# A fused two-block forward pass: compact 32x32 inverse in the scan, packed queries, and a reordered end of the branch stage

## The reference, cut to what matters

```python
# first block, per direction (forward and backward) and head: a scan over tokens
sa = einsum('bhij,bhj->bhi', S, a_t)
S = S * w_t[:, :, None, :] + sa[..., None] * b_t[:, :, None, :] + v_t[..., None] * k_t[:, :, None, :]
y = einsum('bhij,bhj->bhi', S, r_t)
# first block, queries: 8 heads of 64 plain and 32 rotated columns
q = einsum('blr,rf->blf', rms_norm(u_mla[..., :384]), w_uq).reshape(B, L, 8, 96)
q = concatenate([q[..., :64], rope_axial(q[..., 64:], *rot)], -1)
# second block, two layers:
proj = einsum("btd,de->bte", rms_norm(h), w_in[l])        # q k v, indexer, rnn, conv, gates
attn = dsa_attention(...)                                 # top-64 keys per query
rnn  = rg_lru_branch(...)
cnv  = silu(layer_norm(depthwise_conv31(a * sigmoid(g)))) # conformer branch
merged = g_attn*(attn@w_o_attn) + g_rnn*(rnn@w_o_rnn) + g_conv*(cnv@w_o_conv)
h = h + merged @ w_out[l]
h = h + (silu(f@w_gate) * (f@w_up)) @ w_down
```

## Time and profile before

| | |
|---|---|
| median of 3 runs | 1744.97 us (1736.07, 1744.97, 1745.1) |
| the profiled execution | 1739.31 us, its span 1737.5 us |
| mean granted clock of TensorE | 0.985 |
| PE busy | 1675.0 us, 96%, 14722 records |
| DVE busy | 1147.8 us, 66% |
| POOL busy | 661.8 us, 38% |
| ACT busy | 552.7 us, 32% |
| chain that ended last | PE 87%, DVE 6%, ACT 3% |
| largest parts of the chain | L783 18%, L740 16%, L1048 15%, L1072 8%, L2531 5% |

### The profile page before, as it was taken

How to read it: one execution, slowest core, us unless ns; L and a number is a source line. 1 busy time by engine, 2 the same in 40 slices (tenths; PEclk the granted TensorE clock), 3 DMA queues, 4 the chain that set the end, 5 groups by cost and what they waited for, 6 DMA issues and landing times.

```text
span 1737.5 us, 35985 instructions
## 1 busy us (share of the span) xinstructions
PE 1675.0 (96%) x14722; PEld 1480.8 (85%) x14722; DVE 1147.8 (66%) x2044; ACT 552.7 (32%) x1244; POOL 661.8 (38%) x581
## 2 busy tenths in 40 slices
PE   6999988999999999999999999999999998999999
PEld 3777646888889888878989999989888888999999
DVE  5646155665368789787757664368788896676643
ACT  3232363443343453433330010233554304120100
POOL 1535003554035122115645554164123046445652
PEclk9999996999999999999999999999999999999999
DMA  9333100000443444324344444443343343444543
GB/s 371 137 112 115 65 1 2 5 4 5 182 160 122 146 146 146 122 101 142 124 143 173 168 164 158 164 146 128 120 169 127 137 145 107 162 170 170 170 158 110
DMA packets 53379, 225.71 MB, mean 130 GB/s; under 512 B 5088, under 2 KB 29024, under 8 KB 29280
## 3 DMA queue, kind: packets, MB, share of 16 engines
q1 hardware_dynamic: 53216, 223.40, 36.8%
HBM read 222.34 MB, written 1.05 MB: 129 GB/s over the span
## 4 chain that ended last, share of the span: by engine, by line
PE 87%; DVE 6%; ACT 3%; DMA 1%; issue 1%; DVEq 1%; POOL 0%; SPq 0%; ACTq 0%
PE PS L783 18%; PE PS L740 16%; PE PS L1048 15%; PE PS L1072 8%; PE PS L2531 5%; PE PS L2643 3%; PE PS L2060 2%; PE PS L2073 2%; DVE arena L1455 2%; DMA ring<-stream_dram 1%; PE PS L722 1%; PE PS L2736 1%; PE PS L900 1%; PE PS L863 1%; PE PS L1012 1%
## 5 line engine op out<-in xcount | busy, mean ns | idle before, releaser
L783 PE MATMUL PS<-arena,ring 128*128 128x272 f32 (+1 forms) x1664 | 390.0, 389 | 0.3 <-DVE arena L1683 0.3
L783 PEld LDWEIGHTS PS<-arena,ring 128*128 128x128 f32 x1664 | 311.7, 190 | 59.7 <-issue 6.1
L1455 DVE SCALAR_TENSOR_TENSOR arena<-arena,par 128x272 f32<-128x272 f32 (+1 forms) x480 | 259.5, 599 | 7.4 <-issue 0.9
L1895 POOL TENSOR_TENSOR arena<-ring 128x512 f32<-128x512 f32 x48 | 68.7, 1431 | 443.8 <-DMA ring<-stream_dram 353.9
L740 PE MATMUL PS<-arena,ring 128*128 128x136 f32 (+1 forms) x1536 | 202.0, 280 | 1.4 <-ACT arena L1158 1.4
L740 PEld LDWEIGHTS PS<-arena,ring 128*128 128x128 f32 x1536 | 192.7, 191 | 8.1 <-ACT arena L1158 1.7
L740 PE MATMUL PS<-arena 128*128 128x136 f32 (+1 forms) x1152 | 147.9, 280 | 4.5 <-ACT arena L1138 3.0
L1048 PE MATMUL PS<-arena 128*128 128x136 f32 (+1 forms) x1280 | 152.1, 277 | 0.0
L1048 PEld LDWEIGHTS PS<-arena 128*128 128x128 f32 x1280 | 148.7, 191 | 0.0
L740 PEld LDWEIGHTS PS<-arena 128*128 128x128 f32 x1152 | 140.0, 191 | 5.8 <-POOL arena L1895 1.7
L1048 PE MATMUL PS<-arena,ring 128*128 128x136 f32 (+1 forms) x960 | 116.1, 277 | 0.0
(11 more groups left out here) (417 smaller groups left out, 2966.3 us busy)
## 6 DMA issues: line engine op xcount, KB each, us to landing
ring<-stream_dram SPq DMA_DIRECT2D x185, 1024.0 KB, 4.9
ring<-stream_dram SPq DMA_DIRECT2D x32, 512.0 KB, 4.0
ring<-stream_dram SPq DMA_DIRECT2D x16, 384.0 KB, 3.8
arena<-x_dram SPq DMA_DIRECT2D x1, 2048.0 KB, 8.3
cst<-const_dram SPq DMA_DIRECT2D x1, 1080.0 KB, 7.0
out_dram<-H SPq DMA_DIRECT2D x4, 256.0 KB, 3.1
cst<-const_dram SPq DMA_DIRECT2D x1, 912.0 KB, 12.7
arena<-stream_dram SPq DMA_DIRECT2D x1, 512.0 KB, 11.1
```

Of the source, the lines that this page charges most:

```text
L783: last = mm(PS[:, 2 * (j % 2) + f, nw], w[:, k, P * f:P * f + P], src[:, k, nw], start=k == 0, stop=k == KD - 1)
L1455: stt(CVG[:, c, NQ], CVA[:, c, j + Q0:j + T2], dw_w[l][:, c, j:j + 1], CVG[:, c, NQ], ALU.mult, ALU.add)
L1895: g.tensor_tensor(to[:, 0], w21, w22, ALU.add).then_inc(L["summed"], 1)
```

## The change

Three parts.

**Queries**: the eight heads' features are made as two groups of three full 128-row tiles (18 products instead of 24); ACT cuts them into heads with nine copies. The keys come before the swap, the swap's four products go to four different quarters of the partitions of one bank, DVE multiplies them in one instruction, and ACT moves them back. The gate rows and their addition move into the attention loop.

**Scan**: the 64x64 inverse is kept as its two 32x32 diagonal blocks, stored one above the other (ZW has 32 columns). Levels 1 to 4 work on 32x32 tiles, 32 products of 16 columns where 16 of 32 columns were; level 5 makes the corner, and PE copies the second block through an identity (FOLD); the whole inverse is put together in ZF. `grow` is no longer interleaved. `first_products` leaves out a corner that nobody needs.

**Layers**: step 12 becomes a mixed step. The convolution's pieces lie in other steps, with a table for each layer. The attention's token sums move from POOL to DVE (step 35 or 33). The layer norm begins at step 36 in the first layer, 37 in the second; squares, silus and the gains before the feed-forward part are cut in halves and put between the copies on ACT.

```diff
-CONV_SUM_J = 37
-MIXED = [*range(2, 8), 9, 11, 15, ...
-CONV_STEPS = {8: 3, ... 26: 1, 27: 4, 28: 5, 29: 3, 30: 5, 31: 5, 32: 3, 33: 4,
-              34: 4, 35: 5, 36: 1}
+CONV_SUM_J, ATT_SUM_J = (36, 37), (35, 33)
+MIXED = [*range(2, 8), 9, 11, 12, 15, ...
+CONV_STEPS = [{8: 3, ... 26: 1, **late}
+              for late in ({27: 4, 28: 8, 29: 3, 30: 7, 31: 5, 32: 3, 33: 4, 34: 4, 35: 1},
+                           {27: 5, 28: 5, 29: 6, 30: 8, 31: 6, 32: 4, 33: 3, 34: 2})]
...
-        ZW = lend(12, 2, 2, 2, 4, CH)
+        ZW, ZF = lend(12, 2, 2, 2, 4, 32), lend(14, 2, 2, 4, CH)
...
+                    if j == CONV_SUM_J[l] + 1:
+                        square(0)
+                    if j == CONV_SUM_J[l] + 4:
+                        conv_silu(1).then_inc(L["conv_out"], 1)
                     if j - 1 in MIXED:
                         copy_e(j - 1)
+                    if j >= WO_J + 2:
+                        gain(j - 2, (0,))
                     copy_g(j)
...
+                if j == ATT_SUM_J[l]:
+                    dve.wait_ge(L["o_kept"], B["o_kept"] + len(R))
+                    x = AT.rearrange("p (k e) t -> p k e t", e=2)
+                    token_sums(v, x[:, :, 0], x[:, :, 1], TATT, n0, n1).then_inc(L["att_halves"], 1)
...
-                if j == OA_J:
-                    pool.wait_ge(L["o_kept"], B["o_kept"] + len(rounds(l)))
-                    front_halves(pairs(AT), TATT, n0, n1, L["att_halves"])
-                    back_halves(pairs(AT), TATT, n0, n1, L["att_halves"])
...
                 for q, h in each:
-                    last = mm(PS[halves(h), 4 * d, 32 * q:32 * q + 32], XL[l - 1][halves(h), d, q, :],
-                              columns(ZW[halves(h), n % 2, d, 0, q, :], l, GROWN[d]), start=True, stop=True)
+                    if l < 5:
+                        for i in range(2):
+                            o = quad_of(h, i)
+                            last = mm(PS[o, 4 * d, 16 * q:16 * q + 16], XL[l - 1][o, d, q, :],
+                                      columns(ZW[o, n % 2, d, 0, q, :], l, GROWN[d]), start=True, stop=True)
+                    else:
+                        o = quad_of(h, 1 - d)
+                        last = mm(PS[quad_of(h, d), 4 * d, 32 * q:32 * q + 32], AS[n % 2][o, d, q, far(d)],
+                                  ZW[o, n % 2, d, 0, q, :], start=True, stop=True)
...
-                last = mm(PS[halves(h), 4 * d, 256 + 32 * q:288 + 32 * q], ZW[halves(h), n % 2, d, 1, q, :],
-                          P1[halves(h), d, 32 * q:32 * q + 32], start=True, stop=True)
+                n_out = 16 if l < 5 else 32
+                for q, h in each:
+                    for i in range(2):
+                        o, at = quad_of(h, i), slice(n_out * q, n_out * q + n_out)
+                        if l < 5 or i == d:
+                            w, src = ZW[o, n % 2, d, 1, q, :], P1[o, d, at]
+                        else:
+                            w, src = FOLD[o, :], ZW[o, n % 2, d, 0, q, :]
+                        last = mm(PS[o, 4 * d, 256 + at.start:256 + at.stop], w, src, start=True, stop=True)
...
                 for d in range(2):
+                    if n < NCH:
+                        grow(n, l, d)
+                for d in range(2):
                     for q, h in each:
-                        if n < NCH:
-                            grow(n, l, d, q, h)
                         if l == 1 and m >= 0:
                             value(m, d, q, h)
...
-            for i in range(KD):
-                last = mm(PS[:, 7, 2 * i:2 * i + 2], ROWSG[:, i // 2, P * (i % 2):P * (i % 2) + P], SEL, start=True, stop=True)
-            last.then_inc(gate_rows, 1)
...
-            for h in range(8):
-                if h >= 4:
-                    pe.wait_ge(mq_kept, h - 3)
-                for k in range(3):
-                    w = weights(UQ + h // 4, 3, 384)
-                    last = mm(PS[0:96, h % 4, 0:TX], w[:, k, 96 * (h % 4):96 * (h % 4) + 96], REST[:, 4 + k, :],
-                              start=k == 0, stop=k == 2)
+            for i in range(3):
+                for g in range(2):
+                    w = weights(UQ + g, 3, 384)
+                    for k in range(3):
+                        last = mm(PS[:, i, TX * g:TX * g + TX], w[:, k, P * i:P * i + P], REST[:, 4 + k, :],
+                                  start=k == 0, stop=k == 2)
...
+            for i in range(4):
+                last = mm(PS[32 * i:32 * i + 32, 4, :], perm32[64:96, :],
+                          QM[64:96, 2 * i:2 * i + 2, :].rearrange("p h t -> p (h t)"), start=True, stop=True)
```

More of the change, by code:

```diff
@@ L1261, in keep_gates, with square, conv_silu, gain @@
                       ).then_inc(L["ga_kept"], 1)
-            def gain(j):
-                for k in (2 * (j - WO_J), 2 * (j - WO_J) + 1):
+            def square(i):
+                act.wait_ge(L["conv_cent"], B["conv_cent"] + 1)
+                return a(CSQ[:, 4 * i:4 * i + 4, NQ], CVG[:, 4 * i:4 * i + 4, NQ], ACT.Square)
+            def conv_silu(i):
+                act.wait_ge(L["conv_normed"], B["conv_normed"] + 1)
+                for k in range(4 * i, 4 * i + 4):
+                    last = a(CVG[:, k, NQ], CVG[:, k, NQ], ACT.Silu, bias=q2l["ln_b"][:, k:k + 1],
+                             scale=q2l["ln_g"][:, k:k + 1])
+                return last
+            def gain(j, tiles=(0, 1)):
+                for k in (2 * (j - WO_J) + f for f in tiles):
                     act.wait_ge(L["mixed"], B["mixed"] + k + 1)
@@ L2254, in keep_solved, with keep_corner @@
                 last.then_inc(S["u_kept"], 1)
+            def keep_corner(n, d):
+                S = SCAN[d]
+                act.wait_ge(S["z_ready"], 4 * n + 4)
+                for h in range(2):
+                    o = quad_of(h, d)
+                    a(ZF[o, n % 2, d, :, far(d)], ZW[o, n % 2, d, 0], ACT.Copy)
             def keep_turned(n, d):
@@ L2278, in scalar_scan @@
                     if l == 5 and n < NCH:
+                        for d in range(2):
+                            keep_corner(n, d)
                         keep_turned(n, 0)
@@ L2307, in pool_scan @@
                 m = n - 1
-                for l in range(1, 6):
+                for l in range(1, 5):
                     for d in range(2):
@@ L2355, in first_inverse @@
                 dve.wait_ge(S["first_masked"], n + 1)
-                tt(w, w, over(eye, 4), ALU.add).then_inc(S["first_summed"], 1)
+                tt(w, w, over(FOLD, 4), ALU.add).then_inc(S["first_summed"], 1)
             def first_turned(n, d):
@@ L2704, in _ @@
                        start=True, stop=True).then_inc(ms_made, 1)
+                if i == 3:
+                    pe.wait_ge(vt_kept, 4)
+                    for f in range(KD):
+                        last = mm(PS[:, 7, 2 * f:2 * f + 2], ROWSG[:, f // 2, P * (f % 2):P * (f % 2) + P], SEL,
+                                  start=True, stop=True)
+                    last.then_inc(gate_rows, 1)
                 if i >= 3:
@@ L2885, in _ @@
                 a(KM[0:64, h, :], PS[halves(h % 2), h % 4, :], ACT.Copy).then_inc(mk_kept, 1)
+            act.wait_ge(lat_normed, 2)
+            for i in range(4):
+                last = a(PM[64:96, i, :], TURNED[quad[i], :], ACT.Copy)
+            last.then_inc(lat_root, 1)
             for t in range(4):
```

198 lines of the change are left out of this document (108 added, 90 removed).

## The result

The changed kernel takes 1774.28 us (median of 4 runs, 1772.95 to 1777.93), the kernel before 1744.57 (4 runs, 1736.07 to 1745.1). The ratio is 1.0185 with a 95% interval of 1.015 to 1.022: slower by 1.9%, where I had forecast 1703. The mean granted clock fell from 0.985 to 0.960.

The account below looks back on a forecast made before the run. PE was taken as the bound, busy 96% of the span. Queries −7, scan −15 and layers −17 sum to −39 from 1739.31 us, giving 1700 and, 3 us above, forecast 1703; range 1682 to 1741.

Parts of the forecast that it names:

- the scan's sum: Scan: shorter bursts minus growths no longer hidden, over all chunks, −15 us (−28 to +4).
- A pure burst then saves 0.47 us: Scan: one product stage for both directions, not interleaved, falls from 1.12 us to 0.65 us.
- the eight pure bursts: Scan, per chunk: five of level and growth at l=2, 3, 5 together save 3.8 us.
- The bound from above: Scan: a burst of 64 small records takes at most 0.93 us, at 14.5 ns each.
- Rows 2 show it doesn't: Scan: the array does not run empty between 64x64 and 64x128 tiles; the next burst starts 0.07 us early.
- rival (c): Scan: the array runs empty at each tile-size switch, 96 switches at up to 0.165 us, +16 us, 1719; chance 0.05.
- Rival (e): Scan: the clock stays at 1.2 GHz, +70 us, 1773; chance 0.12 in full, 0.05 in part (about 1740).
- Rival (d): Scan: records never start closer than 34 ns, a burst 2.2 us, over 100 us more, about 1820; chance 0.02.
- The queries: Queries to attention: fewer products, a faster swap and hidden gate rows save 7 us (−9 to −4).
- The layers: Two layers: PE's waits at the layer norm go, plus clock and mixed steps, −17 us (−22 to −6).
- (b): Layers: the vector engine is late anew at gates or token sums, so the layers give −6, 1714; chance 0.10.

Follow-up runs that it names:

- wide_products: Changed kernel with one 64-column product replacing four 16-column ones in levels 1 to 4, 3072 records fewer: 1693.41 us, ratio 0.9738.
- columns_filled: wide_products with the 3072 left-out records put back as single-column products on the same tiles: 1774.8 us, ratio 1.0199.
- pair_products: Changed kernel with one 32-column product replacing two of 16 columns in levels 1 to 4: 1718.36 us, ratio 0.9883.
- small_added: Kernel before plus a one-column 32x32 product ahead of each 64x64 one in levels and growths: 2395.46 us, ratio 1.3775.
- switch_added: Kernel before plus one single-column 32x32 product per burst of levels and growths, 160 switches: 1756.09 us, ratio 1.0104.
- crossed_tiles: all_but_scan with the backward direction on off-diagonal 64x64 tiles in levels 2, 3 and (chunks 0 to 4) 5: 1724.15 us, ratio 0.9922.
- all_but_scan: Changed kernel with the old scan, so only the queries' and layers' parts: 1716.12 us, ratio 0.9871 to the kernel before.

## Why the prediction was wrong

**The failing step is the scan's sum.** "A pure burst then saves 0.47 us" priced 64 records by their pace on the array. The pace was right: 11 ns against 10, 0.73 us against 0.65. But ten bursts per chunk with 32 records more each are 320 records, 640 instructions, 2.5 packets of 256, and I costed their arrival at nothing, without naming what hides it. At 3.85 us a packet that is 9.6 us per chunk, against the 3.8 us that the eight pure bursts were to give back; the chunks grew by 7.9 (chunk 1) and 7.0 us (chunk 5). Before, 38 packets at 3.85 us were 146 us, below the scan's 169, and PE's own work was the longer; now 58 are 223 us, and the scan takes 224. The rows for it were in the profile of before: its page counts 118 packets of instructions, 38 of them start in the scan, where two neighbours are never less than 3.3 us apart, and PE already idled for 5 us on issue there. The prediction uses none of them. Even at 3.3 us, the 57 packets of 7280 records are 188 us, and the forecast had the scan at 154.

**The bound from above was none.** I took 14.5 ns from the earlier trace rows; but 65 records in 0.94 us is a rate that holds for half a packet. What a burst can do and what a stretch can sustain are two numbers, 11 and 30 ns here, and only the first was in my sum.

**"Rows 2 show it doesn't" was a misreading** (rival (c), 0.05). A switch does cost, 0.11 us each; this would be worth about 10 us in a version that isn't bound by supply. The count was near: 96 in the prediction, 92 in the traces.

**Rival (e) gave the right number, 1773 us, for a wrong cause.** The clock did fall, for more than half of the scan. But with the same tiles and columns and fewer instructions it stayed up (wide_products), with the instructions alone put back it fell again (columns_filled), and the packets came no faster at 2.4 GHz than at 1.2: its own part in the 55 us is under 8. What brings the clock down stays open. In the new scan the low clock came together with many gaps on issue, but gaps alone do not tell it: pair_products has 25 us of gaps in all, before 9, and both have 28 us at 1.2 GHz; the last chunk of the kernel before and nearly the whole scan of small_added, with 3 us of gaps in 823, are at 1.2 GHz while PE counts as busy.

**Rival (d)** was nearest in kind: a floor per record. It has the wrong form, though: single records start 7 ns apart (median), so 34 ns is no floor from start to start. The Trainium skill's figure that I cited (page "TensorE: Matmul & The Clock Gate", about 25 ns) disagrees with the trace for neighbouring records on several tiles; as a mean over a long stretch of small records, 30 ns, it would have warned me better than the earlier trace rows did.

**The queries** were forecast at -7 (-9 to -4): alone they measure -10 (-13 to -7), by all traces -6.7, the chain's two terms within 0.2 us of their values. **The layers** were forecast at -17 (-22 to -6): alone -14 (-17 to -11), by all traces -13.4. DVE's 42 taps ahead of the gate took 17.86 us, 0.43 each, where 17.6 were expected:

```profile
1414.09 17.86 DVE L1469 SCALAR_TENSOR_TENSOR arena<-arena,par 128x256 f32<-128x256 f32 x42
```

The waits of 6.1 and 2.6 us are gone; that on DVE's sum for a mixed step was to shrink from 1.4 to 0.5 and grew to 2.5 (1.5 in the first layer), since DVE makes four token sums of some 1.6 us each ahead of it. This is (b) in small.

The range ended at 1741 because (e) in full was left outside it; no case had supply as its cause. (Its low end adds up to 1683, not 1682, and 32 records in 1.12 us are 35 ns each, not 34; neither matters here.)

## What to carry to other kernels

Price an edit in instructions as well as in array time: where a change doubles the number of small products, divide the stretch's records by 128 and multiply by the shortest packet interval that the trace shows; if even this lower bound is longer than the stretch you forecast, the forecast is wrong. Idle times on issue that lie a multiple of one packet apart are the sign. Read the cost of a tile switch from start to start of two records, never from the modelled end. And a low clock beside idle times need not be their cause, nor cost the time that it seems to: compare the same interval at either clock before blaming it.

## What the runs showed of the hardware

- PE's instructions come in 16 KB packets of 256, and no stretch of small products sustained more than one per about 3.8 us (3.78 to 3.93 in means of 16 to 29 intervals, at either clock; the shortest single one took 3.3). That is 30 ns for a weight load and matmul, while 64 such records ran in 0.73 us out of what had arrived.
- A switch between 32x32 and 64x64 tiles costs 0.11 us beside a clock of mostly 2.4 GHz (switch_added) and at most 0.26 us at 1.2 GHz (small_added); between 64x64 and 64x128 tiles the start-to-start time is likewise 149 to 202 ns against 21 to 31.
- Products on 64x64 tiles in two places take 31 to 35 ns a record whether 32 or 64 columns pass (L2060, L2131 before), and 14.5 ns when four tiles are in use (crossed_tiles).
- The kernel that is left standing, all_but_scan, runs at 1716.12 us.
